# Ten norms of a one-core block stack: squares and their means slice by slice inside the stage before, root from PSUM, two adjoining norms joined

## What is computed

```python
def rmsnorm(x, g):
    x32 = x.astype(jnp.float32)
    y = x32 * lax.rsqrt(jnp.mean(x32 * x32, axis=-1, keepdims=True) + EPS)
    return (y * g.astype(jnp.float32)).astype(x.dtype)
def modulate(h, shift, scale):
    return h * (1 + scale) + shift
```

## Time and profile before

| | us |
|---|---|
| median of 3 runs | 1786.47 |
| the runs | 1785.82, 1786.47, 1789.46 |
| the profiled execution, its own time | 1788.33 |
| its span in the profile | 1787.0 |
| busy: PE, DVE | 1505.1 (84%), 1293.7 (72%) |
| busy: POOL, ACT | 658.6 (37%), 561.6 (31%) |
| chain that ended last, by engine | PE 55%, DVE 19%, DMA 17%, issue 6%, ACT 2%, POOL 1% |

### The profile page before, as it was taken

The page is one execution under the profiler, slowest core; times in us unless marked ns, Lnnn a source line. Parts: engine busy times, 40 slices in busy tenths (PEclk is TensorE's granted clock), DMA queues, the critical chain, the costliest instruction groups (busy, mean ns, idle before and its releaser), DMA issues.

```text
span 1787.0 us, 21078 instructions
## 1 busy us (share of the span) xinstructions
PE 1505.1 (84%) x7840; PEld 1129.9 (63%) x7840; DVE 1293.7 (72%) x2554; ACT 561.6 (31%) x1049; POOL 658.6 (37%) x475
## 2 busy tenths in 40 slices
PE   1799998999989889999899888788777768777776
PEld 1697678999988789999887678633233223233222
DVE  7974438877789876676656445898888889888665
ACT  5332324444446654444333233311111111111000
POOL 6410002554468024543111112455444435554440
PEclk6789559999999999999898588999999999999999
DMA  8553116777842167777242033699999999999994
GB/s 349 200 234 141 47 48 259 293 285 296 301 170 94 46 240 280 281 274 270 71 165 94 1 130 118 266 418 427 427 427 427 427 427 427 427 427 427 427 427 185
DMA packets 65766, 477.17 MB, mean 267 GB/s; under 512 B 7296, under 2 KB 7296, under 8 KB 8192
## 3 DMA queue, kind: packets, MB, share of 16 engines
q0 software_dynamic: 36864, 268.45, 35.8%
q1 hardware_dynamic: 28512, 205.80, 31.0%
q10 hardware_dynamic: 288, 1.57, 0.2%
HBM read 474.75 MB, written 1.05 MB: 266 GB/s over the span
## 4 chain that ended last, share of the span: by engine, by line
PE 55%; DVE 19%; DMA 17%; issue 6%; ACT 2%; POOL 1%; SPq 0%; DVEq 0%; POOLq 0%; ACTq 0%
DMA ring<-in_uv,acc 9%; PE ps L1469 8%; DMA row<-in_uv,acc 8%; PE ps L1470 8%; PE ps L1471 8%; PE ps L1743 4%; PE ps L1616 3%; PE ps L1618 3%; PE ps L1619 3%; PE ps L1552 3%; PE ps L1634 2%; PE ps L1569 2%; DVE HID L493 2%; DVE ring L945 2%; PE ps L1454 2%
## 5 line engine op out<-in xcount | busy, mean ns | idle before, releaser
L1325 POOL TENSOR_TENSOR WB<-ring,WB 128x1024 fp32r<-128x1024 f32 x72 | 190.1, 2640 | 457.8 <-ACT WB L1021 457.6
L1469 PE MATMUL ps<-hH,WB 128*128 128x256 f32 x1016 | 302.5, 298 | 28.8 <-DVE hL L466 22.8
L1021 ACT ACTIVATE WB<-ring 128x1024 fp32r<-128x1024 f32 x232 | 244.5, 1055 | 205.8 <-PE ps L1619 96.0
L1743 PE MATMUL ps<-ring,P 128*128 128x512 f32 x520 | 243.7, 614 | 72.1 <-DVE P L958 72.1
L1743 PE MATMUL ps<-row,P 128*128 128x512 f32 x504 | 242.3, 627 | 68.7 <-DVE P L958 68.4
L1470 PE MATMUL ps<-hL,WB 128*128 128x256 f32 x1016 | 294.4, 290 | 0.0
L1471 PE MATMUL ps<-hH,WB 128*128 128x256 f32 x1016 | 294.1, 289 | 0.0
L431 DVE TENSOR_TENSOR WB<-ring,WB 128x1024 fp32r<-128x1024 f32 x160 | 206.4, 1291 | 95.6 <-ACT WB L1021 94.4
L1743 PEld LDWEIGHTS ps<-ring,P 128*128 128x128 f32 x520 | 95.8, 193 | 219.0 <-DVE P L958 119.9
L1743 PEld LDWEIGHTS ps<-row,P 128*128 128x128 f32 x504 | 95.2, 197 | 215.1 <-DVE P L958 111.6
L1469 PEld LDWEIGHTS ps<-hH,WB 128*128 128x128 f32 x1016 | 201.6, 198 | 36.5 <-issue 27.6
(11 more groups left out here) (230 smaller groups left out, 2544.7 us busy)
## 6 DMA issues: line engine op xcount, KB each, us to landing
ring<-in_um SPq DMA_DIRECT2D x64, 1024.0 KB, 6.8
ring<-in_ff SPq DMA_DIRECT2D x64, 1024.0 KB, 5.0
ring<-in_w_in SPq DMA_DIRECT2D x24, 1024.0 KB, 4.9
ring<-in_pw SPq DMA_DIRECT2D x12, 1024.0 KB, 4.8
ring<-in_wm SPq DMA_DIRECT2D x8, 1024.0 KB, 13.2
ring<-in_w_out SPq DMA_DIRECT2D x8, 1024.0 KB, 4.9
ring<-in_wq SPq DMA_DIRECT2D x8, 1024.0 KB, 4.8
bias<-in_bias SPq DMA_DIRECT2D x2, 2048.0 KB, 11.7
```

The lines of the kernel that those rows point to most:

```text
L1021: se.activation(unit_dst(j, 0), unit_src(j), ACT.Copy).then_inc(s_hi, 1)
L1325: lo_g.then_inc(ge.tensor_tensor(unit_dst(j, 1), unit_src(j), f(unit_dst(j, 0)), ALU.subtract), j)
L1469: te.matmul(o, wh[:, c], hi[:, kt, :], start=(kt == 0), stop=False)
L1743: mm = te.matmul(ps[4 + 2 * n + q][:, :], diag[:, g % 8, :], row_ap[row_of(g)][:, 1024 + q * 512:1536 + q * 512], start=(g % 128 == 0), st ...
```

## The change

It does the following.

- **Squares and means slice by slice.** `squares(n)` becomes `square(n, kt)`, `moments(n)` becomes `mean_square(n, kt)`. For mlp0, mlp1 and ffn ACT squares slice u right after its `ahead` of tile u in w_out, pw2 and w_out2; PE takes the mean of slice u-1 (in pw2: u-2) behind tile u. For conv and for b2 and fin ACT squares two slices after each unit of ff2's last block, and PE takes their means a unit later. The others keep eight in a row.
- **Root from PSUM.** ACT takes the square root of the mean straight from PSUM with EPS as bias; DVE's step (L443) goes, and so does the same kind of step in the gating (L519), whose 1/128 becomes the activation's scale.
- **An extra root** (`sqrt_next`): a root of one column, before the last Squares of a stage.
- **rows2**: the first two tiles after a norm (mlp0, conv, pw2, mlp1, b2, ffn) go slice by slice together: six matmuls a slice, into both banks.
- **fin and b2 as one.** b2's statistic is taken from the unscaled x with squares scaled by the root of final_g² + EPS, into ps[0], beside fin's in ps[2]; norm b2 uses a column multiplied by final_g. fin's eight products come after norm b2.
- **ln**: product and lo alternate with a distance of two instead of eight products and then eight lo.
- Small constants (eps, fgs), one wait changed from r_raw to r_done.

The diff, cut to its core:

```diff
 emptying, totals = [], {}
 
 xsrc = {"x0": xT, "ctx": cT, "mlp0": xT, "conv": xT, "ln": yc, "mlp1": xT, "fin": xT, "b2": xT, "ffn": xT}
+moment_bank = {n: ps[2][:, 0:256] for n in norms} | {"b2": ps[0][:, 0:256]}
...
         return s_cen, k + 1
     if n == "mlp1":
         return x_done["pw2", k]
-    if n == "fin":
+    if n in ("fin", "b2"):
         return x_done["mlp1", k]
-    if n == "b2":
-        return x_done["fin", k]
     return out_v["w_out2", k // 4, k % 4, 0]
 
...
         for _ in range(beside[i]):
             mods(i)
 
-    def rstd(n, src, scale=1.0):
-        r = rr[:, norms.index(n) % 2, :]
-        V.wait_ge(*moment[n])
-        r_raw.then_inc(ve.tensor_scalar(r, src, scale, EPS, ALU.mult, ALU.add), n)
-        return r
-
-    def root(n):
+    def rstd(n):
         r = rr[:, norms.index(n) % 2, :]
         V.wait_ge(*r_root[n])
-        V.then_inc(ve.reciprocal(r, r))
+        r_done.then_inc(ve.reciprocal(r, r), n)
+        V.wait_ge(*r_done[n])
+        return r
 
     def affine(i, layer, half, g):
         V.then_inc(ve.scalar_tensor_tensor(out=ab[:, i, :], in0=M[:, layer, 24 * half + 8:24 * half + 16],
                                            scalar=1.0, in1=g, op0=ALU.add, op1=ALU.mult))
 
-    def norm(n, a, b):
+    def norm(n, a, b, r):
         src, (hi, lo) = xsrc[n], hbuf[n]
-        r = rr[:, norms.index(n) % 2, :]
         V.wait_own()
         for kt in range(10):
             if kt < 8:
...
-            root("x0")
+            r0_ = rstd("x0")
         slot, turn = wm0_at(kt)
         V.wait_ge(s_slot[slot], 16 * turn)
         if kt == 0:
...
         n = f"mlp{l}"
         have_mod(l, 4)
         affine(i_ab, l, 1, g)
-        rstd(n, ps[2][:, 0:256])
-        root(n)
-        norm(n, ab[:, i_ab, :], M[:, l, 24:32])
...
     V.wait_ge(*y_v[CV[-1]])
     for kt in range(8):
         ve.tensor_tensor(yc[:, kt, :], yc[:, kt, :], ps[7][:, 0:256], ALU.subtract).then_inc(s_cen, 1)
-    r = rstd("ln", ps[2][:, 0:256])
-    root("ln")
-    V.wait_own()
-    for kt in range(8):
-        ve.scalar_tensor_tensor(out=yc[:, kt, :], in0=yc[:, kt, :], scalar=col["lcg"][:, kt:kt + 1], in1=r,
-                                op0=ALU.mult, op1=ALU.mult).then_inc(s_ln, 1)
-    for kt in range(8):
-        V.wait_ge(s_yh, kt + 1)
-        ve.tensor_tensor(XL[:, kt, :], yc[:, kt, :], f(XH[:, kt, :]), ALU.subtract).then_inc(s_yl, 1)
+    r = rstd("ln")
+    for kt in range(10):
+        if kt < 8:
+            ve.scalar_tensor_tensor(out=yc[:, kt, :], in0=yc[:, kt, :], scalar=col["lcg"][:, kt:kt + 1], in1=r,
+                                    op0=ALU.mult, op1=ALU.mult).then_inc(s_ln, 1)
+        if kt >= 2:
+            k = kt - 2
...
     mlp(1, 3, col["ng"][:, 24:32])
 
 
-    r = rstd("fin", ps[2][:, 0:256])
-    root("fin")
+
+    have_mod(2, 1)
+    affine(4, 2, 0, col["na"])
     V.wait_own()
+    V.then_inc(ve.tensor_tensor(ab[:, 3, :], ab[:, 4, :], col["fg"], ALU.mult))
+    norm("b2", ab[:, 3, :], M[:, 2, 0:8], rstd("b2"))
+    r1 = rstd("fin")
     for kt in range(8):
         x_done.then_inc(ve.scalar_tensor_tensor(out=xT[:, kt, :], in0=xT[:, kt, :], scalar=col["fg"][:, kt:kt + 1],
-                                                in1=r, op0=ALU.mult, op1=ALU.mult), ("fin", kt))
-    have_mod(2, 1)
-    affine(4, 2, 0, col["na"])
-    rstd("b2", ps[2][:, 0:256])
-    root("b2")
-    norm("b2", ab[:, 4, :], M[:, 2, 0:8])
+                                                in1=r1, op0=ALU.mult, op1=ALU.mult), ("fin", kt))
...
                 S.wait_ge(*dense[used[j - 3]])
             se.activation(unit_dst(j, 0), unit_src(j), ACT.Copy).then_inc(s_hi, 1)
 
-    def squares(n):
-        for kt in range(8):
-            S.wait_ge(*x_ready(n, kt))
-            squared.then_inc(se.activation(sq[:, kt, :], xsrc[n][:, kt, :], ACT.Square), (n, kt))
+    def square(n, kt):
+        S.wait_ge(*x_ready(n, kt))
+        g = {"scale": fgs[:, kt:kt + 1]} if n == "b2" else {}
+        squared.then_inc(se.activation(sq2[:, kt, :] if n == "b2" else sq[:, kt, :], xsrc[n][:, kt, :], ACT.Square, **g), (n, kt))
 
     def root(n):
-        r = rr[:, norms.index(n) % 2, :]
-        S.wait_ge(*r_raw[n])
-        r_root.then_inc(se.activation(r, r, ACT.Sqrt), n)
+        k = 1 if n == "ik" else 2 if n == "b2" else 0
+        S.wait_ge(*moment[n])
+        S.wait_ge(s_eps, 4)
+        r_root.then_inc(se.activation(rr[:, norms.index(n) % 2, :], moment_bank[n], ACT.Sqrt, bias=eps[:, k:k + 1]), n)
+
+    def sqrt_next():
+
+        se.activation(eps[:, 3:4], eps[:, 0:1], ACT.Sqrt)
...
     for b in range(2):
         for u in range(4):
             ahead(first["w_out", b] + u)
+            if (b, u) == (1, 3):
+                sqrt_next()
+            square("mlp0", 4 * b + u)
+    root("mlp0")
 
     def mlp(l):
         n = f"mlp{l}"
-        squares(n)
-        root(n)
         norm(n, M[:, l, 24:32])
         tails = []
 
...
                     ahead(first[f"ff2_{l}", s - 1] + u)
                     if u == 0:
                         tail()
+                    if s == 8:
+                        if u == 3:
+                            sqrt_next()
+                        for kt in (2 * u, 2 * u + 1):
+                            for n in (("conv",) if l == 0 else ("b2", "fin")):
+                                square(n, kt)
 
     mlp(0)
-
-    squares("conv")
     root("conv")
     norm("conv", M[:, 1, 0:8])
     for s in range(4):
...
             S.wait_ge(*dense[name])
             out_a.then_inc(se.activation(ptmp[:, kt, :], row_bank(name)[:, 0:256], ACT.Identity,
                                          bias=ab[:, 4, kt:kt + 1], scale=M[:, 1, 16 + kt:17 + kt]), name)
+            if kt == 7:
+                sqrt_next()
+            square("mlp1", kt)
+    root("mlp1")
 
     mlp(1)
-    squares("fin")
+    root("b2")
     root("fin")
-    squares("b2")
-    root("b2")
     norm("b2", M[:, 2, 0:8])
     i0 = first["w_in2", 6]
...
         for g in totals.get(place, ()):
             total(g)
 
-    def moments(n):
-        for kt in range(8):
-            T.wait_ge(*squared[n, kt])
-            mm = te.matmul(ps[2][:, 0:256], onesn[:], sq[:, kt, :], start=(kt == 0), stop=(kt == 7))
-        moment.then_inc(mm, n)
+    def mean_square(n, kt):
+        T.wait_ge(*squared[n, kt])
+        mm = te.matmul(moment_bank[n], onesn[:], (sq2 if n == "b2" else sq)[:, kt, :], start=(kt == 0), stop=(kt == 7))
+        if kt == 7:
+            moment.then_inc(mm, n)
 
...
             te.matmul(o, wh[:, c], lo[:, kt, :], start=False, stop=False)
             mm = te.matmul(o, wl[:, c], hi[:, kt, :], start=False, stop=(kt == 7))
         dense.then_inc(mm, name)
+
+    def rows2(i, names, ready, hl):
+
+        hi, lo = hl
+        for d, name in enumerate(names):
+            T.wait_ge(*lo_of(i + d))
+            T.wait_ge(s_hi, i + d + 1)
+            if row_at[name] >= 2:
+                T.wait_ge(*empty(row_tiles[row_at[name] - 2]))
+        for kt in range(8):
+            T.wait_ge(*ready(kt))
+            c = slice(kt * 128, kt * 128 + 128)
+            for d, name in enumerate(names):
+                wh, wl = WB[:, (i + d) % 3, 0, :], WB[:, (i + d) % 3, 1, :]
+                o = row_bank(name)[:, 0:256]
+                te.matmul(o, wh[:, c], hi[:, kt, :], start=(kt == 0), stop=False)
+                te.matmul(o, wh[:, c], lo[:, kt, :], start=False, stop=False)
+                mm = te.matmul(o, wl[:, c], hi[:, kt, :], start=False, stop=(kt == 7))
+                if kt == 7:
+                    dense.then_inc(mm, name)
 
...
             i = first["w_out", b] + u
             rows(i, ("w_out", b, u, 0), lambda kt: cat_l["A", 1], (XH, XL))
             totals_at(i)
+            if 4 * b + u:
+                mean_square("mlp0", 4 * b + u - 1)
+    mean_square("mlp0", 7)
 
     def mlp(l):
         n = f"mlp{l}"
-        moments(n)
         for s in range(9):
             if s < 8:
                 for u in range(4):
                     i = first[f"ff1_{l}", s] + u
+                    if (s, u) == (0, 0):
+                        rows2(i, [(f"ff1_{l}", 0, 0, 0), (f"ff1_{l}", 0, 1, 0)], normed(n), (hH, hL))
+                        totals_at(i)
+                        totals_at(i + 1)
+                    if (s, u) in ((0, 0), (0, 1)):
+                        continue
                     rows(i, (f"ff1_{l}", s, u, 0), normed(n), (hH, hL))
                     totals_at(i)
             if s:
...
                                            skip_group_check=True)
                     dense.then_inc(mm, (f"ff2_{l}", d, u))
                     totals_at(i)
+                    if d == 7 and u:
+                        means_after_mlp(l, u - 1)
+        means_after_mlp(l, 3)
+
+    def means_after_mlp(l, u):
+        for kt in (2 * u, 2 * u + 1):
+            for n in (("conv",) if l == 0 else ("b2", "fin")):
+                mean_square(n, kt)
 
     mlp(0)
-    moments("conv")
```

(8 more changed lines are left out.)

101 lines of the change are left out of this document (62 added, 39 removed).

## The result

| us | before | after |
|---|---|---|
| median (runs) | 1787.23 (1785.82 to 1789.46, 4 runs) | 1811.68 (1809.78 to 1813.34, 4 runs) |
| ratio, 95% interval | | 1.0135 [1.0118, 1.0153] |
| span of the profiled execution | 1787.0 | 1812.0 |

What follows compares the result with a forecast made beforehand. Dense stages were taken as bound by PE, with norms as gaps whose changes shift everything behind, gathers included. Terms for ctx, mlp0, conv, mlp1, fin/b2 and ffn summed to +7.7 us, giving 1794.2; own range 1790 to 1799, 8-in-10 range 1785 to 1801.

Steps and rivals of the forecast that it cites:

- the rings: w_out and pw2: residual or addition, Square, hi, lo, modulation step in a circle, 4.2 us a tile; +4.6 and +5.1.
- Rival 1: w_out and pw2: Square and residual fit in ACT's idle time, hi not late; 1780.5 to 1782.9 us, chance 0.10.
- rival 3: w_out and pw2: the rings cost half, as L415 is shorter beside less POOL work; 1789.3 us, chance 0.08.
- the modulation step: DVE's L415, part of the ring: 1.20 us usually, 3.03 beside unit 7's lo on POOL in w_out.
- One sign: w_out and pw2, expected in the changed profile: PE waits up to 0.9 us a tile.
- the joined norms: fin and b2 as one: b2's first matmul 5.9 us earlier, but third tile waits for DVE; -3.3 kept.
- Table load: ACT's 1.28 us load before the root: hidden behind the means, so preloading gives 0.
- root from PSUM: Every norm: dropping DVE's L443 and a handoff saves 0.46 us together; ctx gains only this, -0.4.
- the step in x0: L443 dropped from DVE's chain of first products in x0: taken as 0, with -0.9 us as bound.
- the first one: Whole kernel: dense stages run at PE's pace, a norm's gain or loss shifts everything behind equally, gathers included.
- Conv's pair: First two tiles of conv taken together slice by slice: priced at -0.1 us.
- the clock behind fin: PE's wait before the third b2 tile may cost clock in the tiles behind it: bound +1.8 us.

Runs made afterwards that it cites:

- e1: Changed kernel with its two small tensors put into unused columns of older ones, so tensors behind keep their old addresses: 1800.83 us, ratio to before 1.007.
- e2: Kernel before with an unused 48-byte tensor (per partition) where the change puts its two small tensors; no instruction differs: 1796.86 us, ratio 1.0054.
- f2: Changed kernel with small tensors in unused columns, Squares one tile later, fin's products behind w_in2's first eight tiles, all pairs kept: 1786.74 us, ratio to before 0.9993.
- f3: Like f2 but with no tiles taken in pairs: 1784.79 us, ratio to the kernel before 0.9986.
- g1: Like f2 but without the pairs of conv and wq: 1782.77 us, ratio to the kernel before 0.9972.
- e3: Changed kernel with 16 more unused bytes a partition behind its two small tensors, 64 in all: 1808.56 us.
- g4: Kernel before with only the sixteen Squares of mlp0 and mlp1 moved, each behind its own tile of w_out or pw2: 1797.12 us, ratio 1.0048.
- e4: Changed kernel with each Square of w_out, pw2 and w_out2 one tile later in ACT's order: 1797.96 us, ratio to before 1.0054.

## Why the prediction was right and wrong

**Right: the rings.** The 4.2 us a turn, the seven turns of pw2 (28.8 forecast, 28.9 measured), forecast +4.6 and +5.1, together 9.7, measured +3.9 and +5.8 in the changed kernel, also 9.7, and 9.6 in the total of the Squares moved alone. Rival 1, the hidden ring, is refuted, and so is rival 3 as a whole. That the two stages come out at exactly the sum is in part luck: 0.7 us too much in w_out, 0.7 too little in pw2. The part from the last residual to the first matmul was 6.3 us rather than 5.7. In w_out the full turns are 4.2 to 4.3 as forecast, but one was short: the modulation step that I had at 3.03 us, beside POOL's low part, now ran ahead of that part (278.60 against 280.17) and took 1.28, and residual 5 followed residual 4 by 1.6 us (278.21, 279.80) instead of 3.4. So residual 7 stands 31.0 us after the first w_out matmul, where I had 31.8. One sign was wrong: PE does not wait up to 0.9 us in each tile, it waits 2.7 and 3.5 us at the end of pw2.

**Right: the joined norms**, within about 1 us. b2's first matmul comes 4.9 us earlier from mlp1 (forecast 5.1), and the eight products do hold the third tile. In the changed kernel's own profile they took 5.34 us, because one of them took 2.57, and the wait was 5.62; in e1's they took 3.26, as before, and the third tile started 10.74 us after the first, forecast 10.9. PE and DVE of e1 there:

```profile
866.18 0.55 PE L1496 MATMUL ps<-hH,WB 128*128 128x256 f32 x1 [3.72 <-DVE hL L464]
876.92 0.38 PE L1477 MATMUL ps<-hH,WB 128*128 128x256 f32 x1 [2.11 <-DVE WB L434]
```

```profile
872.48 3.26 DVE L770 SCALAR_TENSOR_TENSOR xT<-xT,cols,rr 128x256 f32<-128x256 f32 x8
875.65 1.22 DVE L434 TENSOR_TENSOR WB<-ring,WB 128x1024 fp32r<-128x1024 f32 x1
```

The next block is 3.5 us later from b2, not 2.6, so of the gain 1.4 us were kept and not 3.3. Table load, root from PSUM and the step in x0 were costed at nothing or 0.4, and no run took these out alone.

**Wrong: the gather stage.** The step that failed is the first one: "what a norm gains or loses moves everything behind it, the gather stage too, by the same amount". I had read its DMA share of 0.96 and taken from a saturated stage that it can only be shifted. A saturated stage (DMA share 1.01 in both kernels) is the one where the rate itself is the time, and I never asked what the change does to it. I had counted added and removed instructions, and the two small tensors got no step at all; their cost was put at nothing without a reason. They put 48 bytes ahead of the destinations of 268 MB: 9.3 us in the changed kernel, gone in e1, where they alone are taken away, and there again in e2, where they alone are added. Without them the time is at the upper edge of the range (1800.8).

**Wrong: small terms, 5 us together, nearly all the same way.** In the table of stages they are: mlp1 +0.7, mlp1 to b2 +0.2, behind b2 +0.9, conv +1.1, w_out2 +0.2, wq +2.6, less 0.6 for mlp0 with its stage. Conv's pair was priced -0.1; f2 against f3 and g1 gives it a cost of 1.5 to 1.8. The pairs were priced from a start at half clock, and the trace of the kernel before shows that start: in mlp0 the granted clock is 0.50 from 291.0 to 296.0 us, with neighbouring matmuls 0.21 to 0.22 us apart, and 1.00 from 296.2 on, with 0.12. In wq I gave the pair -0.5 for the slices. But the copy of tile 1, for which the first key scores wait, now comes late, and a stretch at a granted clock of 0.50 became longer, 10.2 us (1118.5 to 1128.7) where it was 6.8 (1105.0 to 1111.9), as worked out from windows of 2 us. PE's waits in wq (in total, times, longest), changed kernel; the longest was 0.7 us before:

```profile
PE ps L1791 <- DVE HID L470: 2.2, 2, 1.6
```

Windows over the second half of wq, kernel before and changed kernel, nearly the same number of matmuls in each, PEclk is the number behind POOL's:

```profile
1109.80:1138.10 28.30, 26.20 (x205) 25.47 (x204) 19.22 (x50) 10.96 (x19) 11.47 (x8) 0.96 0.29 101
```

```profile
1123.60:1153.30 29.70, 27.58 (x206) 26.85 (x205) 19.03 (x50) 10.94 (x19) 11.47 (x8) 0.91 0.26 93
```

0.96 became 0.91 and 28.3 us became 29.7. Why the clock stays low for longer behind the same idle gap (1.88 us up to 1103.48 before, 1.87 up to 1117.13 after) I haven't isolated: the second half of wq takes 29.0 to 29.7 us in every version with the change but g1 (28.6), with the pair and without, and 28.3 to 28.5 in the six profiles without the change. The bounds had 1.8 us for the clock behind fin and nothing for it elsewhere.

**The time.** By the means of the profiles the change costs 13.3 us up to the gathers and 9.3 in them, 22.6 of the 24.5. In the two profiled executions themselves the parts are -0.9 ahead of w_out, +16.0, +9.3 and +0.5 behind the last gather, 25.0 in all. The 3 us by which the changed kernel's own profile lies above those of e1 and e3, with the same instructions, are not explained; most of them lie behind b2 (0.7 us up to w_in2's block 0, then 1.0 and 0.8 in the two stages that follow). The terms that I had would have given 1794.2, and with 9.3 us for the gathers 1803.5, with the small terms some 1809; e1, the change without its 48 bytes, has 1800.8 and is 0.7% slower where 0.4% was forecast.

## What to carry to other kernels

An operation put into an engine's program costs what waits behind it (9.6 us for the sixteen Squares of g4): give it a place where its input is already there, as the Squares had one tile later in e4. Small tensors go into unused columns of older ones, as in e1 (behind the large ones was not tried), and after any change to the allocations compare the rate of the transfers that fill the saturated stage (427 and 421 GB/s here), not only the instructions. Work that is joined or paired has to be followed to its next consumer (the third tile, the first copy), which is where a good part of the gain was given back.
